# Value pages of a paged attention: issued from GpSimd's queue instead of SP's

## The reference

```python
def mla_attend_paged(q_lat, q_rope, ckv, k_rope, pool_lat, pool_rope, page_table):
    past_lat = pool_lat[page_table].reshape(DB, -1, R)          # R = 128
    past_rope = pool_rope[page_table].reshape(DB, -1, MLA_ROPE)
    s_past = einsum('bqhr,bkr->bhqk', q_lat, past_lat) + einsum('bqhd,bkd->bhqk', q_rope, past_rope)
    ...
    p = jax.nn.softmax(s, axis=-1)
    return einsum('bhqk,bkr->bqhr', p_past, past_lat) + einsum('bhqk,bkr->bqhr', p_new, ckv)
```

## Time and profile before

| | |
|---|---|
| median of 3 executions | 1704.53 us (1701.05 to 1709.95) |
| the profiled execution's own time | 1707.16 us |
| its span (first to last instruction) | 1705.2 us |
| mean granted clock of TensorE | 0.900 of full speed |
| busy: PE, PEld, DVE, ACT, POOL | 90%, 82%, 52%, 30%, 1% |
| DMA: moved, mean rate | 147.36 MB, 86 GB/s |
| DMA time of 16 engines: SP's queue, GpSimd's queue | 26.3%, 1.9% |

### The profile page before, as it was taken

The page is one execution under the profiler, slowest core; times in us unless marked ns, Lnnn a source line. Parts: engine busy times, 40 slices in busy tenths (PEclk is TensorE's granted clock), DMA queues, the critical chain, the costliest instruction groups (busy, mean ns, idle before and its releaser), DMA issues. The chain is left out here.

```text
span 1705.2 us, 28473 instructions
## 1 busy us (share of the span) xinstructions
PE 1538.7 (90%) x11052; PEld 1390.7 (82%) x11052; DVE 882.7 (52%) x1454; ACT 518.4 (30%) x768; POOL 24.4 (1%) x49
## 2 busy tenths in 40 slices
PE   4988798778999999999999888878898999999993
PEld 4988475446999999999998876545598999999993
DVE  4584142433566643666665713343346666356664
ACT  3341013332343322333424201232324333233341
POOL 1000000000000000000000000000000000000001
PEclk9996567889999999999999855778999999999996
DMA  7410223123323223222362022212232232333231
GB/s 277 118 56 24 76 59 85 39 71 102 97 75 95 80 87 112 87 87 77 104 205 76 15 66 62 72 52 75 75 112 70 92 100 75 97 102 89 71 93 50
DMA packets 119463, 147.36 MB, mean 86 GB/s; under 512 B 16609, under 2 KB 90626, under 8 KB 119202
## 3 DMA queue, kind: packets, MB, share of 16 engines
q1 hardware_dynamic: 116114, 133.54, 26.3%
q0 software_dynamic: 3216, 12.00, 1.9%
HBM read 141.24 MB, written 4.45 MB: 85 GB/s over the span
## 5 line engine op out<-in xcount | busy, mean ns | idle before, releaser
L1230 PE MATMUL PS<-XNH,WH 128*128 128x260 f32 x2176 | 443.9, 285 | 41.6 <-DVE WL L739 21.3
L1230 PE MATMUL PS<-XNH,WL 128*128 128x260 f32 x2176 | 441.3, 285 | 0.0
L1230 PE MATMUL PS<-XNL,WH 128*128 128x260 f32 x2176 | 440.6, 284 | 0.0
L1230 PEld LDWEIGHTS PS<-XNH,WH 128*128 128x128 f32 x2176 | 337.5, 189 | 45.8 <-issue 33.2
L452 ACT ACTIVATE WH<-RAW 128x1024 fp32r<-128x1024 f32 x200 | 211.5, 1057 | 475.9 <-PE PS L1230 401.8
L1230 PEld LDWEIGHTS PS<-XNH,WL 128*128 128x128 f32 x2176 | 337.1, 189 | 0.3
L1230 PEld LDWEIGHTS PS<-XNL,WH 128*128 128x128 f32 x2176 | 336.3, 189 | 0.4
L739 DVE TENSOR_TENSOR WL<-RAW,WH 128x1024 fp32r<-128x1024 f32 x200 | 244.7, 1223 | 169.8 <-ACT WH L452 169.0
L1230 PE MATMUL PS<-HL,WH 128*128 128x260 f32 x704 | 141.9, 283 | 0.0
L1230 PE MATMUL PS<-HH,WL 128*128 128x260 f32 x704 | 141.5, 282 | 0.0
L1230 PE MATMUL PS<-HH,WH 128*128 128x260 f32 x704 | 141.3, 282 | 0.0
(11 more groups left out here) (246 smaller groups left out, 1446.5 us busy)
## 6 DMA issues: line engine op xcount, KB each, us to landing
RAW<-in_units SPq DMA_DIRECT2D x134, 512.0 KB, 3.6
KT<-in_kat SPq DMA_DIRECT2D x256, 64.0 KB, 1.8
KT<-in_ka SPq DMA_DIRECT2D x256, 64.0 KB, 1.8
RAW<-in_units SPq DMA_DIRECT2D x32, 384.0 KB, 3.1
RAW<-in_units SPq DMA_DIRECT2D x32, 320.0 KB, 2.9
RT<-in_kar SPq DMA_DIRECT2D x256, 16.0 KB, 1.7
C<-in_const POOLq DMA_DIRECT2D x1, 2228.0 KB, 10.1
X<-in_x SPq DMA_DIRECT2D x8, 260.0 KB, 3.7
```

The lines of the kernel that those rows point to most:

```text
L1230: last = mm(PS[i % 4][0:rows, hb, 0:HB], w, x(kk)[:, hb * HB:(hb + 1) * HB], start=(kk == 0 and s == 0), stop=(kk == total - 1 and s == 2))
```

## The change

The 128 value-page transfers of each layer, with the loads of their page numbers, leave SP's queue and stand in GpSimd's, behind the store `out_sret` and ahead of `out_ff`. They keep their order (sequence by sequence, page by page), their size and the wait on `pages_used[s]` with the same counts. They count on semaphores of their own, `vals_in[s]`, and PE's `dp` steps wait on those; the counts of `pages_in[s]` now hold keys and rotary keys alone. Where SP's page numbers come through a helper with a register offset into the table, the new loads have constant offsets.

```diff
--- before.py
+++ after.py
@@ -239,6 +239,7 @@
         full_s = [sem(f"full{i}") for i in range(4)]
         emptied_s = [sem(f"emptied{i}") for i in range(4)]
         pages_in = [sem(f"pages_in{i}") for i in range(2)]
+        vals_in = [sem(f"vals_in{i}") for i in range(2)]
         pages_used = [sem(f"pages_used{i}") for i in range(2)]
         names = {"sq_ready": 5, "sq_used": SQ_MID[-1], "std_ready": 6, "xf_ready": 0, "xsq_ready": 16, "xsq_added": 16, "xh_ready": 16, "xl_ready": 16,
                  "mid_used": 16, "roped": 6, "cq_normed": 3, "kr_roped": 1, "zeroed": 1, "acc_zero": 1,
@@ -366,8 +367,6 @@
                         four_pages(l, 0, 0, g // 4, 4 * (g % 4))
                 for bp in range(NB // 2 - 1):
                     pages(l, 0, bp + 1)
-                for bp in range(NB // 2):
-                    pages(l, 1, bp)
                 wait_full(sp, l, "dy")
                 settle(sp)
                 for u in range(N_IN_U + 2, U_UP[0]):
@@ -422,6 +421,19 @@
                 wait_emptied(pool, l, "du")
                 settle(pool)
                 pool.dma_start(sret_o[bass.ds(l, 1)].rearrange("a p k n -> p (a k) n"), SD[:, :, :]).then_inc(saved, 16)
+                pool.wait_ge(pt_clamped, 1)
+                for b in range(NB):
+                    s = b % 2
+                    pool.wait_ge(pages_used[s], l * NB + NB // 2 + b // 2 + CREDIT)
+                    for j0 in range(0, N_PAGES, 4):
+                        _, numbers = nc.values_load_multi_w_load_instructions(
+                            PT_SB[0:1, b * N_PAGES + j0:b * N_PAGES + j0 + 4], engines=[mybir.EngineType.Pool],
+                            min_val=0, max_val=N_PHYS - 1,
+                            skip_runtime_bounds_check_because="Vector has clamped the page numbers to the pool")
+                        for j, page in enumerate(numbers, j0):
+                            pool.dma_start(KT[:, s, j * P:(j + 1) * P],
+                                           kav[bass.ds(l * N_PHYS + page, 1), :, :].rearrange("a p n -> p (a n)"))\
+                                .then_inc(vals_in[s], 16)
                 wait(pool, "fout_ready", l, NJ)
                 pool.dma_start(ff_o[bass.ds(l, 1)].rearrange("a p k n -> p (a k) n"), FOUT[:, :, :]).then_inc(saved, 16)
                 wait(pool, "saved", l, 16 * 11)
@@ -1335,7 +1347,7 @@
                                   start=False, stop=j % 4 == 3)
                     last.then_inc(full(name), 1)
 
-                per_layer = 16 * (3 * N_PAGES) * (NB // 2)
+                per_layer = 16 * (2 * N_PAGES) * (NB // 2)
                 page_scores(0)
                 page_scores(1)
 
@@ -1500,7 +1512,7 @@
                             s = b % 2
                             plain(pe)
                             wait_tile(pe, l, name)
-                            pe.wait_ge(pages_in[s], l * per_layer + (NB // 2) * 16 * 2 * N_PAGES + (b // 2 + 1) * 16 * N_PAGES)
+                            pe.wait_ge(vals_in[s], (l * (NB // 2) + b // 2 + 1) * 16 * N_PAGES)
                             settle(pe)
                             mm(ps(name)[0:MH, 0, 0:P], SMALL[0:NB, 1, MH * b:MH * b + MH], C8[:, :], start=True, stop=False)
                             for j in range(N_PAGES):
```

## The result

The changed kernel took 1719.72 us in the median of 6 executions (1718.11 to 1726.81), the kernel before 1706.13 us beside it (6 executions, 1701.05 to 1709.95). The ratio is 1.0087, 95% interval 1.0064 to 1.0111: slower by some 14 us, which is under 1%, but the interval does not reach 1. 1702 us had been forecast. The profiled execution took 1718.11 us, with a span of 1716.5 us and a mean granted clock of 0.897.

A forecast was written before the change was run, and what follows sets the result against it. PE's waits for the 32-page chain before `dp7` were taken as the stake: 1707.16 us profiled, less 2.55 gain, plus 0.3, is 1704.9; that execution being 2.63 above the median, 1702 was forecast, range 1697 to 1717.

The forecast's parts named there:

- What bounds the kernel: PE's waits before `dp6` and `dp7`: the chain of 32 value pages sets the attention's end twice; 3.7 us at most recoverable.
- the reading of GpSimd's queue: GpSimd's sequencer spends about 0.28 us on a transfer, its own work per page is 0.54, about the engine's; 0.54 taken.
- the break-even with SP: In the 32 pages ahead of `dp7`: the series rival decides from a GpSimd page of 0.62 us, SP's cost there.
- The delay in the chain: One delay of 1.0 us allowed per GpSimd chain, since one of SP's page issues once took 1.29.
- The first page: On GpSimd after the slot's release: load 0.30, registers 0.07, transfer 0.57, together 0.94 us (SP: 0.6).
- The landing: A 64 KB page from GpSimd's queue lands in 2.0 us, against 1.8 for SP's pages.
- The series rival: GpSimd's 32 pages ahead of `dp7` cost 0.80 us each, unhidden; 1716 us; chance 0.17, plus 0.09 for above that.
- VectorE in GpSimd's way: Four `PR` scalings hold up GpSimd in the chain, 1.5 us longer per layer; gain gone, 1705 us; chance 0.10.
- What runs earlier: First slot's values start beside SP's last key pages, ahead of `ds7`; 0.3 us cost taken in the first layer, bounds 0 to 1.

The follow-up runs named there:

- run 2: Changed kernel with constant page numbers on GpSimd, so no number loads or register work; 1706.47 us, ratio 0.9987 to the kernel before.
- run 5: Changed kernel with values of sequences 0 and 1 back on SP, 2 to 7 on GpSimd; 1719.35 us, ratio 1.0053 to the kernel before.
- run 6: Changed kernel with values of sequences 6 and 7 back on SP, 0 to 5 on GpSimd; 1716.05 us, ratio 1.0048 to the kernel before.
- run 7: Changed kernel with only sequence 7's values on GpSimd, all others on SP; 1709.50 us, ratio 1.0018 to the kernel before.
- run 9: Kernel before, values on SP, with 96 small copies per layer added on GpSimd; 1713.02 against 1707.21 us, ratio 1.0038.
- run 8: Changed kernel with 32 small copies more per layer on GpSimd ahead of the first value page; 1719.87 us, ratio 1.0061 to the kernel before.
- run 3: Changed kernel with values of odd sequences on GpSimd, even ones on SP; 1706.91 us, ratio 0.9995 to the kernel before.
- run 11: Kernel before with odd sequences' values on GpSimd, even ones on SP, and the stores of y on SP; 1697.38 us, ratio 0.9932.
- run 10: Kernel before with the eight stores of y issued by SP instead of GpSimd; 1700.39 us, ratio 0.9958.

## Why the prediction was wrong

**What bounds the kernel** was right: the chain of 32 pages ahead of `dp7` sets the end of the attention, twice, and its length decided.

**The step that failed** is the reading of GpSimd's queue: "So the sequencer spends about 0.28 on a transfer before it goes on, and not 0.53". It came from the time between VectorE's end and the start of `out_ret`, which tells how soon a transfer starts, and not when the sequencer is free again. The rows of line 434, and of the loads in line 429, show the latter (queue instructions and the transfer, ns, first and last start; landing in us):

```profile
L434 POOLq FUSED_REGOPS  x256: 37/46/56, 273.3 to 1242.3; - x128
L434 POOLq MOVE KT<-in_ka x256: 29/29/29, 273.4 to 1242.4; - x128
L434 POOL DMA_DIRECT2D KT<-in_ka x256: 534/534/742, 274.0 to 1242.9; - x128
...
DMA to landing us min/median/max: 1.9/2.1/2.8
```

```profile
L429 POOLq TENSOR_LOAD <-PT_SB x64: 314/319/530, 272.7 to 1240.2; - x64
```

The last page's register work is at 1242.3, half a microsecond ahead of its own transfer at 1242.9 and right at the start of the one before, 1242.9 - 0.58 = 1242.3. So the sequencer goes through register work in 0.08 and then stands some 0.5 in the transfer; both add, 0.58, and a load of four numbers adds 0.40, 0.10 a page. In the prediction's own terms: some 0.5 in place of 0.28 for the transfer, 0.08 in place of 0.19 for the register work, 0.10 in place of 0.075 for the load. I forecast 0.54 and measured 0.67; run 2, without that work, has 0.54. I had put the break-even with SP at 0.62.

**The delay in the chain** was put at 1.0 us, from SP's single long issue; it is 2.77 and 2.78, always after the same page. **The first page** after the release was put at 0.94 and took 382.33 - 381.3 = 1.0. **The landing** was put at 2.0 and is 2.1. In the first layer `dp7` started 27.6 us after the release, where the sum had its pages in after 20.7: of the 6.9 us the pace is 4.0 (31 x 0.13), the pause 1.7 more than the 1.0 put in for it, and the rest small gaps, the first page and the landing.

**The series rival** was right in its total, not in its parts: it put `dp7`'s pages at 27.7 us after the release, and PE started at 408.87, 27.6 after it. But the page costs 0.67, not 0.80; the pause and the small gaps fill the rest. The time it gave, 1716, was short because I priced only the waits. That PE comes out of a longer wait at a lower granted clock, 7.5 us over the four steps, was in no term.

**VectorE in GpSimd's way** did not happen to any extent that counts. In run 5 a scaling of `PR` ran beside the chain:

```profile
401.09 1.27 DVE L1055 TENSOR_SCALAR PR<-PR,STAT 128x128 f32<-128x128 f32 x4
```

The four pages from 399.35 took 2.40 instead of 2.28 us, and the next gap was 0.28 instead of 0.40, so nothing was lost. By the rule of the Trainium skill, page "DMA: Bandwidth & Descriptors", section "SWDGE vs HWDGE vs iDMA", descriptor writing should have been held up there; the trace shows 0.12 us. In the second layer of run 5 a step between two pages, 1.12 us instead of 0.59, falls on such a scaling (1232.95 to 1234.22). It comes after the queue's 214th transfer, and run 6 has the same step after its 214th, where no scaling runs. In the changed kernel a scaling falls into the pause of both layers (394.79 and 1230.87), but in run 2 the pause (391.4 to 394.1) is over before the scaling begins:

```profile
395.42 1.33 DVE L1048 TENSOR_SCALAR PR<-PR,STAT 128x128 f32<-128x128 f32 x4
```

**What runs earlier** cost nothing: `ds7` waited 2.07 us for ScalarE, as before (2.06 in the earlier trace rows), and run 2, whose pages start as early, has no loss.

**The end of the program** was in no step. In the changed kernel it helped by 1.6 us (drain 2.11 instead of 3.74); in the mixed kernels of runs 5 to 7 the drain is 2.6 to 5.7 us longer.

**Open:** what sets the pause. It is not the number of instructions (run 2), not VectorE (run 2), not the bytes (runs 5, 6 and 9), not a plain count of transfers or row descriptors (run 8), and it does not belong to the chain (runs 3, 5, 6, 9 and 11). Each kernel whose GpSimd queue carried 165 transfers or more has one or two such gaps, the first after 120 to 131 transfers, in run 8 after 163; those with 37, 45 and 77 have none. Open too is why the stretches between came out 2 us shorter each in the changed kernel's profile; they differ as much between kernels that share this code.

## What to carry to other kernels

Moving transfers to an idle queue gains only if that queue can issue them at the pace of the old one: take the pace from rows with the same address work, and where none exists, take the time to the next register instruction, not the time from a release to the transfer's start. A wait of PE costs more than its length when the products behind it run at a lower granted clock, so price the first step behind it too. And look at what the queues do after the last result: stores at the end belong on the queue whose closing drain is short.

## What the runs showed that I had not expected

- GpSimd's closing drain grows with the transfers that its queue has carried, as long as there are few: 3.08 us for 37 (run 10), 3.74 for 45 (before), 6.36 for 77 (run 7), 0.083 each. Beyond that it is not proportional: 6.68 for 165 (run 11), 7.34 for 173 (run 3), 9.46 for 237, whatever their size (runs 5, 6, 9), and 2.11 for 301 and for 365 (the changed kernel and run 8). All of these had paused. Counted from the last pause, 24 transfers in the changed kernel and run 8 would give 2.0 us and the 111 of runs 5, 6 and 9 would give 9.2, which fits; 53 in run 3 and 45 in run 11 would give 4.4 and 3.7, which does not. That the pause clears what the drain would have to clear is not shown.
- SP's own closing drain, behind the same eight stores, took 0.007 us in run 10.
